# Softmax attention's front moved between the weight slots of the input projection

## What is computed

```python
h = rms_norm(x, attn_pre_g[l])
proj = h @ w_in[l]                       # 3080 columns
qa, ka, va, qb, kb, vb, f_logit = jnp.split(proj, split_at, axis=-1)   # 6 x 512, then 8
qa, ka = partial_rotary(qa, cos, sin), partial_rotary(ka, cos, sin)
oa = diff_attention(qa, ka, va, lam)     # 4 heads, two softmaxes each, joined with lam
log_f = jax.nn.log_sigmoid(f_logit + forget_bias[l])
ob = forgetting_attention(qb, kb, vb, log_f)   # 8 heads; logits + cumsum(log_f)_q - cumsum(log_f)_k
x = x + rms_norm(concat(rms_norm(oa), ob) @ w_out[l], attn_post_g[l])
```

## Time and profile before

| | us |
|---|---|
| median of 3 runs | 2193.26 |
| lowest, highest | 2191.91, 2195.44 |
| the profiled execution | 2196.09 |
| its span in the trace | 2194.3 |
| outside the span | 1.8 |
| mean granted TensorE clock | 0.997 |

### The profile page before, as it was taken

How to read it: one execution, slowest core, us unless ns; L and a number is a source line. 1 busy time by engine, 2 the same in 40 slices (tenths; PEclk the granted TensorE clock), 3 DMA queues, 4 the chain that set the end, 5 groups by cost and what they waited for, 6 DMA issues and landing times.

```text
span 2194.3 us, 27783 instructions
## 1 busy us (share of the span) xinstructions
PE 2125.9 (97%) x10508; PEld 1758.4 (80%) x10508; DVE 778.9 (35%) x1496; ACT 749.1 (34%) x1279; POOL 848.6 (39%) x390
## 2 busy tenths in 40 slices
PE   7999999999999999999999999998989999999999
PEld 5877788888887886798888887776777789888887
DVE  5217542121005117542121005587567543121200
ACT  4226452222224136452222224454433434222211
POOL 3430035444444430134444434333444344444442
PEclk9999999999999999999999999999999999999999
DMA  6320023333233320023333322211111232333232
GB/s 195 96 96 1 1 87 114 97 96 96 96 90 102 96 86 1 1 90 114 98 98 98 97 87 59 77 50 47 58 48 49 80 113 82 101 96 96 87 101 72
DMA packets 138738, 178.25 MB, mean 81 GB/s; under 512 B 19856, under 2 KB 87696, under 8 KB 138640
## 3 DMA queue, kind: packets, MB, share of 16 engines
q1 hardware_dynamic: 137024, 175.25, 26.3%
q10 hardware_dynamic: 1616, 1.64, 0.2%
HBM read 174.76 MB, written 2.10 MB: 81 GB/s over the span
## 4 chain that ended last, share of the span: by engine, by line
PE 38%; issue 33%; POOL 17%; DVE 9%; ACT 3%; POOLq 0%; ACTq 0%; DVEq 0%
POOL w_lo L557 17%; PE PS L1465 9%; PE PS L1467 8%; PE PS L1466 8%; PE PS L1728 3%; PE PS L1740 2%; PE PS L1859 1%; DVE R L1374 1%; PE PS L1716 1%; DVE R2R L1311 1%; PE PS L1667 1%; DVE R L1382 1%; PE PS L1834 1%; PE PS L1826 0%; DVE R L1370 0%
## 5 line engine op out<-in xcount | busy, mean ns | idle before, releaser
L557 POOL TENSOR_TENSOR w_lo<-R,w_hi 128x1024 fp32r<-128x1024 f32 (+1 forms) x288 | 678.9, 2361 | 956.8 <-ACT w_hi L638 907.0
L638 ACT ACTIVATE w_hi<-R 128x1024 fp32r<-128x1024 f32 (+1 forms) x288 | 299.4, 1042 | 966.7 <-PE PS L1467 954.5
L1465 PE MATMUL PS<-xt_hi,w_hi 128*128 128x512 f32 (+1 forms) x1216 | 458.4, 377 | 0.0
L1467 PE MATMUL PS<-xt_hi,w_lo 128*128 128x512 f32 (+1 forms) x1216 | 453.0, 372 | 0.0
L1466 PE MATMUL PS<-xt_lo,w_hi 128*128 128x512 f32 (+1 forms) x1216 | 452.8, 372 | 0.0
L1465 PE MATMUL PS<-w_hi,xt_hi 128*128 128x512 f32 x928 | 375.6, 405 | 16.7 <-DVE R L1275 7.2
L1467 PE MATMUL PS<-w_hi,xt_lo 128*128 128x512 f32 x928 | 364.1, 392 | 0.0
L1466 PE MATMUL PS<-w_lo,xt_hi 128*128 128x512 f32 x928 | 363.4, 392 | 0.0
L1466 PEld LDWEIGHTS PS<-xt_lo,w_hi 128*128 128x128 f32 x1216 | 229.1, 188 | 40.4 <-issue 1.0
L1465 PEld LDWEIGHTS PS<-xt_hi,w_hi 128*128 128x128 f32 x1216 | 229.1, 188 | 40.4 <-issue 1.0
L1467 PEld LDWEIGHTS PS<-xt_hi,w_lo 128*128 128x128 f32 x1216 | 229.0, 188 | 40.4
(11 more groups left out here) (240 smaller groups left out, 2137.6 us busy)
## 6 DMA issues: line engine op xcount, KB each, us to landing
R<-in_w_in SPq DMA_DIRECT2D x56, 512.0 KB, 3.8
R<-in_w_gate SPq DMA_DIRECT2D x88, 256.0 KB, 2.8
R<-in_w_up SPq DMA_DIRECT2D x88, 256.0 KB, 3.0
R<-in_w_down SPq DMA_DIRECT2D x40, 512.0 KB, 3.8
raw<-in_w_in SPq DMA_DIRECT2D x36, 512.0 KB, 3.6
R<-in_w_out SPq DMA_DIRECT2D x24, 512.0 KB, 3.8
R<-in_w_ffn_gate SPq DMA_DIRECT2D x44, 256.0 KB, 2.8
R<-in_w_ffn_up SPq DMA_DIRECT2D x44, 256.0 KB, 3.1
```

The costliest lines, as they stand in the source:

```text
L557: nc.gpsimd.tensor_tensor(w_lo[:, r, 0:subs, :], raw_of(stage, lap)[:, r, 0:subs, :], w_hi[:, r, 0:subs, :].bitcast(F32), ALU.subtract).th ...
L638: nc.scalar.activation(w_hi[:, r, 0:subs, :], raw_of(stage, lap)[:, r, 0:subs, :], ACT.Copy).then_inc(hi_ready, 1)
L1465: mm(out_, a_hi, b_hi, start=start, stop=False)
L1467: return mm(out_, a_lo, b_hi, start=False, stop=stop)
```

## The change

PE's loop over chunks 2 to 5 is written out, and a table `IN_PLAN` names for each chunk which jobs PE does ahead of which of its eight row blocks `k`. The gate logits stand in chunk 2, their turning and the sums in chunk 3, items 0 to 3 (qa) in chunk 2, items 4 to 7 (ka) in chunk 3, items 8 to 15 (qb) in chunk 4 and items 16 to 19 (four heads of kb) in chunk 5. Items 20 to 23 stay behind the projection: two come in the softmax loop after the scores of unit 1 and two after those of unit 2 (`UNIT_ITEMS`). `items1` is reordered, and each item has a fixed bank (`ITEM_BANK`) in the four that the chunk in progress doesn't fill. ACT and DVE copy the items between their other work. vb is copied out by ACT behind its last weight slot, not by DVE. Items 20 to 23 wait for that copy (`evac[1]`), since they use its banks 4 to 7. Buffers move: turned keys of heads 4 to 7 and `prob`, `probT` now lie where the projection's activations were.

```diff
+        ITEM_BANK = [4, 5, 6, 7, 1, 2, 3, 1, 4, 5, 6, 7, 4, 5, 6, 7, 0, 1, 2, 3, 4, 5, 6, 7]
+        AFTER_ITEM = {7: 4, 12: 8, 13: 9, 14: 10, 15: 11}
+        IN_PLAN = {2: {4: [0, 1], 5: [2, 3], 7: ["logits"]}, 3: {2: ["turn", 4, 5], 3: [6], 5: [7], 6: ["sums"]},
+                   4: {2: [8, 9], 3: [10, 11], 5: [12, 13], 6: [14, 15]}, 5: {2: [16, 17], 3: [18, 19]}}
+        UNIT_ITEMS = {2: [20, 21], 3: [22, 23]}
...
-                with act.Fori(2 if l == 0 else 1, LAPS[stage]) as lap:
-                    hi_lap(stage, LAP0[stage] + lap)
-                hi_first(f"out{l}")
...
+                hi_slots(3, [0, 1])
+                turned(0, 2)
+                hi_slots(3, [2])
                 act.wait_ge(f_mm, l + 1)
-                nc.scalar.activation(f_rows, PS[0:16, 0, :], ACT.Copy).then_inc(f_copied, 1)
+                nc.scalar.activation(f_rows, PS[0:16, LOGIT_BANK, :], ACT.Copy).then_inc(f_copied, 1)
+                hi_slots(3, [3])
+                hi_slots(4, [0])
+                turned(4, 6)
+                hi_slots(4, [1])
                 act.wait_ge(f_biased, l + 1)
...
+                hi_first(f"out{l}", [0])
+                turned(16, 18)
+                hi_first(f"out{l}", [1, 2, 3])
+                act.wait_ge(w_used, 4 * (LAP0[stage] + 5) + 4)
+                nc.scalar.activation(VB[:, :, :, 0:HD], PS[:, 4:8, :].rearrange("p t (h d) -> p t h d", h=8),
+                                     ACT.Copy).then_inc(evac[1], 1)
...
+                turned(5)
                 dve.wait_ge(f_log, l + 1)
                 V.scalar_tensor_tensor(fy[:, 2], fy[:, 0], 0.0, fy[:, 1], ALU.min, ALU.subtract).then_inc(f_gate, 1)
+                turned(7)
...
+                chunk_done(stage, 3)
+                V.tensor_copy(QB[:, :, :, 0:HD], heads(banks(1), 8)).then_inc(evac[1], 1)
+                turned(9, 11, 13, 15)
+                chunk_done(stage, 4)
+                V.tensor_copy(KB[:, :, :, 0:HD], heads(banks(0), 8)).then_inc(evac[0], 1)
+                turned(17, 19)
...
                         for sub in range(subs):
+                            for job in plan.get(k, ()):
+                                attention_job(l, job)
...
+                    if u + 1 in UNIT_ITEMS:
+                        if u + 1 == 2:
+                            pe.wait_ge(evac[1], SET0[stage][1] + 3)
+                        for n in UNIT_ITEMS[u + 1]:
+                            attention_item(l, n)
+                    if u + 1 == TURN:
+                        items_turned(l, len(items1))
```

More of the change, by code:

```diff
@@ L1112, in attention1, with turned @@
                 stage = f"in{l}"
-                dst = (QA, KA, None, QB[:, :, :, 0:HD], KB[:, :, :, 0:HD], VB[:, :, :, 0:HD])
-                for c in range(6):
-                    chunk_done(stage, c)
[L1116 to L1130, removed]
+                def turned(*items):
+                    for n in items:
+                        src, rows, to, scale = items1[n]
+                        bank = PS[0:rows, ITEM_BANK[n], :]
+                        dve.wait_ge(tr_mm, len(items1) * l + n + 1)
+                        if isinstance(to, list):
+                            V.tensor_scalar(to[0], bank, scale[:, 0:1], None, ALU.mult)
+                            to, scale = to[1], scale[:, 1:2]
+                        V.tensor_scalar(to, bank, scale, None, ALU.mult).then_inc(tr_dve, 1)
@@ new lines, in attention1 @@
+                for c in range(2):
+                    chunk_done(stage, c)
+                    link(V.tensor_copy((QA, KA)[c], banks(c)))
+                    V.memset(mark[:, c:c + 1], 1.0).then_inc(evac[c], 1)
+                    if l == 0 and c == 0:
+                        dve.wait_ge(trig_done, 1)
+                    rotary((QA, KA)[c])
+                    V.memset(mark[:, 2:3], 1.0).then_inc(rotated, 1)
+                turned(1, 3)
+                chunk_done(stage, 2)
+                V.tensor_copy(VA, banks(0)).then_inc(evac[0], 1)
@@ L1668, in transpose_item, with items_turned, attention_item @@
                 last.then_inc(tr_mm, 1)
+            def items_turned(l, n):
+                pe.wait_ge(tr_act, (len(items1) * l + n) // 2)
+                pe.wait_ge(tr_dve, (len(items1) * l + n) // 2)
+            def attention_item(l, n):
+                src, rows, _, _ = items1[n]
+                if n in AFTER_ITEM:
+                    m = len(items1) * l + AFTER_ITEM[n]
+                    pe.wait_ge(tr_dve if m % 2 else tr_act, m // 2 + 1)
+                for t in range(T):
+                    last = nc.tensor.transpose(PS[0:rows, ITEM_BANK[n], t * P:(t + 1) * P], src[:, t, :], ident[:, :])
+                last.then_inc(tr_mm, 1)
@@ L1670, in attention1 @@
             def attention1(l):
                 stage = f"in{l}"
-                pe.wait_ge(evac[0], SET0[stage][0] + 3)
-                pe.wait_ge(fw_done, 1)
-                for k in range(KD):
-                    mm(PS[0:16, 0, :], fw[:, l, k, :], xt_hi[:, k, :], start=k == 0, stop=False)
-                    last = mm(PS[0:16, 0, :], fw[:, l, k, :], xt_lo[:, k, :], start=False, stop=k == KD - 1)
-                last.then_inc(f_mm, 1)
-                pe.wait_ge(evac[1], SET0[stage][1] + 3)
@@ L1691, in attention1 @@
-                pe.wait_ge(f_gate, l + 1)
-                mm(PS[:, 0, 0:8 * T], SUMS[:, UPTO, :], fy[:, 2, :, :], start=True, stop=False)
-                for back in range(1, T):
-                    last = mm(PS[:, 0, 8 * back:8 * T], SUMS[:, ONES, :], fy[:, 2, 0:T - back, :],
-                              start=False, stop=back == T - 1)
-                last.then_inc(c_mm, 1)
-                pe.wait_ge(c_placed, l + 1)
-                for n in range(8, len(items1)):
-                    transpose_item(n, base, items1, 2 + n % 6, 6)
```

149 lines of the change are left out of this document (94 added, 55 removed).

## The result

| | before | changed |
|---|---|---|
| median of 20 runs each | 2194.19 us | 2197.57 us |
| lowest, highest | 2191.67, 2197.01 | 2194.99, 2200.01 |
| ratio, 95% interval | | 1.0014 [1.0008, 1.0021] |
| span of the profiled execution | 2194.3 | 2195.7 |

The changed kernel is 3.4 us slower, with an interval of 1.8 to 4.6 us. It was timed twice more beside the experiments: 1.0019 [1.0010, 1.0027] and 1.0016 [1.0006, 1.0026]. So it is slower, by less than 0.2% in all three medians.

A forecast was written before the change was run, and what follows sets the result against it. PE, busy 97%, was taken as the bound. First scores 3.55 us earlier, then 4.7 later: +1.15 a layer, +2.3 for two, plus 1.4 for one clock fall, on 2193.26 gave 2197.0 us; range 2191 to 2200.5.

The follow-up runs named there:

- e3: The changed kernel with ACT instead of DVE copying items 21 and 23; 2197.48 us, ratio 1.0016 to before.
- e4: The changed kernel with an extra copy of 1,024 elements that nobody reads on ACT ahead of the copy of vb; 2201.43 us, ratio 1.0027 to before.
- e7: The changed kernel once more, unedited; one of two repeats, which measured 1.0019 and 1.0016 to before.
- e1: The changed kernel with three extra float32 products on PE filling its wait for the copy of vb; 2197.31 us, ratio 1.0011 to before.
- e11: The changed kernel once more, unedited; the other of two repeats, which measured 1.0019 and 1.0016 to before.

## What to carry to other kernels

When work leaves a serial stretch for a covered one, look at what was hidden under that stretch: here ACT's last rounding and the copy of vb cost nothing while PE turned queries and keys, and 2.36 us of idle once they were first in line. Order the copy that the next engine waits for ahead of housekeeping, put work that has no reader yet behind the first units, and cut what must move into a tight loop so small that each piece fits a gap: 1.06 us in one piece cost 0.57, in two pieces 0.14. The second piece stood one head later, so how much is due to the size and how much to the place was not taken apart.

## What the runs showed of the hardware

- The same idle of 2.36 us was followed by the lower clock in two layers of six in the changed kernel, and in neither layer of e3. In e4, with 3.28 us, it fell in both, in layer 1 only more than 1 us after PE had gone on (827.40; the window from 828.00 still has 1.00, that from 829.00 has 0.50). In the second block of the changed kernel's first execution it fell behind an idle of 2.03 us (1565.08) and not behind one of 2.43 (1511.58). Which of its two levels follows an idle of this size is not settled by its length alone.
- At about 42.5 us, in the first chunks of layer 0, PE waits for POOL's low part of a weight slot, between 0.39 and 3.93 us from one execution to another, in whatever kernel. Behind the waits of 2.46 (e7), 2.71 (e1), 2.85 (e3), 3.40 (e11) and 3.93 us (before) the windows show 0.50, behind that of 2.41 (changed) and the shorter ones 1.00. The end of chunk 1 moves with it, between 64.1 and 68.1, by as much as the change under study, so spans of single executions can't be compared here.
